# Opening of a hybrid decoder step: the first weights in two quarters, and four token transfers issued later

## The reference, cut to what matters

```python
a = rmsnorm(h, norm_mix_g)                       # h: tokens x 1024
z = a @ w_in                                     # q, k, v, gates of two branches
hm = mlstm_scan(...); hg = gla_scan(...)         # matrix memory || gated linear attention
merged = sigmoid(ga) * (hm @ w_pa) + sigmoid(gb) * (hg @ w_pb)
h = h + merged @ w_o
h = h + conv_ffn(rmsnorm(h, norm_ffn_g))         # gated FFN, width-3 causal convolution
h = h + sigmoid(rmsnorm(h, norm_ple_g) @ w_ple_gate) * (p @ w_ple_proj)
y = rmsnorm(h, final_norm_g)
```

## Time and profile before

| | us |
|---|---|
| median of three runs | 1183.09 (1182.69 to 1183.25) |
| the profiled execution | 1183.06 |
| its span | 1181.2 |
| busy PE / DVE / ACT | 1166.8 / 757.9 / 393.1 |
| first product of unit 0 | 7.90 |
| first product of unit 1 | 23.98 |

### The profile page before, as it was taken

The page is one execution under the profiler, slowest core; times in us unless marked ns, Lnnn a source line. Parts: engine busy times, 40 slices in busy tenths (PEclk is TensorE's granted clock), DMA queues, the critical chain, the costliest instruction groups (busy, mean ns, idle before and its releaser), DMA issues.

```text
span 1181.2 us, 21812 instructions
## 1 busy us (share of the span) xinstructions
PE 1166.8 (99%) x9169; PEld 1110.0 (94%) x9169; DVE 757.9 (64%) x1396; ACT 393.1 (33%) x576; POOL 2.3 (0%) x7
## 2 busy tenths in 40 slices
PE   9999999999999999999999999999999999999996
PEld 8999999999999999999999999999999999999995
DVE  6855568675777655664655667777777763333777
ACT  6243232134343322333343233333333322111544
POOL 0000000000000000000000000000000000000000
PEclk9999999999999999999999999999999999999998
DMA  6342232422312366563443542232222143223222
GB/s 220 112 145 90 90 108 90 144 72 93 113 67 109 133 228 212 177 199 120 153 155 114 172 147 72 72 108 72 75 105 72 61 163 107 72 94 98 77 99 81
DMA packets 48962, 138.56 MB, mean 117 GB/s; under 512 B 5460, under 2 KB 25108, under 8 KB 39776
## 3 DMA queue, kind: packets, MB, share of 16 engines
q1 hardware_dynamic: 16392, 89.39, 21.9%
q10 hardware_dynamic: 32472, 47.77, 12.0%
HBM read 113.15 MB, written 23.81 MB: 116 GB/s over the span
## 4 chain that ended last, share of the span: by engine, by line
PE 95%; issue 3%; DVE 1%; DMA 1%; ACT 1%; POOL 0%; ACTq 0%; POOLq 0%; DVEq 0%
PE ps L768 34%; PE ps L796 10%; PE ps L794 6%; PE ps L797 6%; PE ps L795 6%; PE ps L897 6%; PE ps L774 6%; PE ps L798 5%; PE ps L903 3%; PE ps L815 2%; PE aux L1060 1%; DMA xT<-in_xT 1%; PE aux L1124 1%; PE aux L955 1%; PE aux L1020 1%
## 5 line engine op out<-in xcount | busy, mean ns | idle before, releaser
L768 PE MATMUL ps<-apair,whi 128*128 128x288 f32 x1728 | 274.9, 298 | 0.6 <-ACT mq L2067 0.5
L768 PEld LDWEIGHTS ps<-apair,whi 128*128 128x128 f32 x1728 | 243.2, 188 | 4.9 <-issue 2.1
L1175 DVE TENSOR_TENSOR wlo<-wraw,whi 128x2048 fp32r<-128x2048 f32 (+1 forms) x82 | 176.1, 2147 | 74.8 <-ACT whi L1912 70.5
L1912 ACT ACTIVATE whi<-wraw 128x2048 fp32r<-128x2048 f32 (+1 forms) x87 | 156.4, 1797 | 106.2 <-PE ps L798 52.5
L796 PE MATMUL ps<-apair,whi 128*128 128x512 f32 x336 | 132.1, 393 | 0.0
L794 PE MATMUL ps<-apair,whi 128*128 128x320 f32 x336 | 105.0, 313 | 0.0
L797 PE MATMUL ps<-apair,wlo 128*128 128x320 f32 x336 | 104.2, 310 | 0.0
L795 PE MATMUL ps<-apair,whi 128*128 128x320 f32 x336 | 103.8, 309 | 0.0
L768 PE MATMUL ps<-apair,wlo 128*128 128x288 f32 x448 | 95.9, 296 | 0.0
L798 PE MATMUL ps<-apair,wlo 128*128 128x256 f32 x336 | 95.1, 283 | 0.0
L798 PEld LDWEIGHTS ps<-apair,wlo 128*128 128x128 f32 x336 | 63.2, 188 | 14.2
(11 more groups left out here) (405 smaller groups left out, 2091.5 us busy)
## 6 DMA issues: line engine op xcount, KB each, us to landing
wraw<-in_w_in SPq DMA_DIRECT2D x31, 1024.0 KB, 4.9
wraw<-in_w_up SPq DMA_DIRECT2D x21, 1024.0 KB, 4.8
gate_scratch<-stg ACTq DMA_DIRECT2D x32, 288.0 KB, 2.8
gt<-gate_scratch ACTq DMA_DIRECT2D x32, 288.0 KB, 2.9
wraw<-in_w_pgate SPq DMA_DIRECT2D x6, 1024.0 KB, 4.8
wraw<-in_w_down SPq DMA_DIRECT2D x8, 704.0 KB, 4.1
wraw<-in_w_down SPq DMA_DIRECT2D x8, 640.0 KB, 3.8
out_C_s<-st ACTq DMA_DIRECT2D x16, 256.0 KB, 2.8
```

Source lines behind the costliest of these rows:

```text
L768: mm = nc.tensor.matmul(ps[:, t % 2, a, 0:HALF], w, x(k)[:, a * HALF:(a + 1) * HALF], start=f, stop=e)
L1175: V.tensor_tensor(wlo[:, s, 0:n], wraw[:, s, 0:n], f32(whi[:, s, 0:n]), ALU.subtract)\
L1912: A.activation(whi[:, s, 0:n], wraw[:, s, 0:n], ACT.Copy).then_inc(split_hi, 1)
```

## The change

The first half of unit 0 arrives in two quarters. The first quarter (blocks 0 and 1, 256 KB) is SyncE's first transfer, ahead of the gains; the second (blocks 2 and 3) follows the gains. VectorE rounds the first quarter itself, before it waits for the gains; ScalarE rounds the second quarter behind block 1. The low parts of the quarters are made by VectorE behind blocks 0 and 1. ScalarE's queue issues only the first token piece ahead of the Sqrt with its table load, and the other four behind it. In `first_unit` TensorE takes the four products with `ahi` before the four with `alo`, and waits for `alo` only between them; it waits for the second quarter at block 2.

```diff
--- before.py
+++ after.py
@@ -431,8 +431,9 @@
             return [sem(f"{name}{i}") for i in range(n)]
 
         raw_in = sems("raw_in", 2)
-        raw_first = sem("raw_first")
+        raw_first = sems("raw_first", 2)
         hi_first = sem("hi_first")
+        hi_second = sem("hi_second")
         lo_first = sem("lo_first")
         ones_set = sem("ones_set")
         misc_in = sem("misc_in")
@@ -582,6 +583,10 @@
             x, k0 = both[0 if k < 4 else 1 if k < 6 else 2]
             return x[:, k - k0, :]
 
+        def quarter(q):
+
+            return slice(q * UW // 4, (q + 1) * UW // 4)
+
         def half_of(e):
             return slice(TS * e, TS * (e + 1))
 
@@ -615,7 +620,6 @@
 
         @block.sync
         def _(sp):
-            sp.dma_start(gains[:, :, :], ins["gains"]).then_inc(gains_in, 16)
             for u, (kind, i) in enumerate(units):
                 s = u % 2
                 if (kind, i) == ("ga", 0):
@@ -633,7 +637,9 @@
                     sp.wait_ge(split_hi, u - 1)
                     sp.wait_ge(split_lo, u - 1)
                 if u == 0:
-                    sp.dma_start(wraw[:, 0, 0:UW // 2], ins["w_in"][0, :, 0:UW // 2]).then_inc(raw_first, 16)
+                    sp.dma_start(wraw[:, 0, quarter(0)], ins["w_in"][0, :, quarter(0)]).then_inc(raw_first[0], 16)
+                    sp.dma_start(gains[:, :, :], ins["gains"]).then_inc(gains_in, 16)
+                    sp.dma_start(wraw[:, 0, quarter(1)], ins["w_in"][0, :, quarter(1)]).then_inc(raw_first[1], 16)
                     sp.dma_start(wraw[:, 0, UW // 2:], ins["w_in"][0, :, UW // 2:]).then_inc(raw_in[0], 16)
                     sp.dma_start(misc_raw[:, :, :], ins["w_misc"]).then_inc(misc_in, 16)
                 else:
@@ -832,20 +838,21 @@
                 for k in range(KT):
                     if k == 0:
                         pe.wait_ge(hi_first, 1)
+                    elif k == 2:
+                        pe.wait_ge(hi_second, 1)
                     elif k == KT // 2:
                         pe.wait_ge(split_hi, 1)
                         pe.wait_ge(split_lo, 1)
-                    pe.wait_ge(a_hi, k + 1)
-                    pe.wait_ge(a_lo, k + 1)
-                    for n in range(2):
-                        col = (2 * k + n) * P
-                        for x in (ahi, alo):
+                    for x, ready in ((ahi, a_hi), (alo, a_lo)):
+                        pe.wait_ge(ready, k + 1)
+                        for n in range(2):
+                            col = (2 * k + n) * P
                             for a in range(2):
                                 nc.tensor.matmul(ps[:, t + n, a, 0:HALF], whi[:, 0, col:col + P],
                                                  x[:, k, a * HALF:(a + 1) * HALF],
                                                  start=k == 0 and x is ahi, stop=False)
-                    if k == 0:
-                        pe.wait_ge(lo_first, 1)
+                    if k in (0, 2):
+                        pe.wait_ge(lo_first, k // 2 + 1)
                     for n in range(2):
                         col = (2 * k + n) * P
                         for a in range(2):
@@ -1467,14 +1474,16 @@
             for s in sched:
                 j, t = job_at[s], tile_at.get(s)
                 if s[0] == "norm_in":
+                    dve.wait_ge(raw_first[0], 16)
+                    V.tensor_copy(whi[:, 0, quarter(0)], wraw[:, 0, quarter(0)]).then_inc(hi_first, 1)
                     dve.wait_ge(gains_in, 16)
                     for k in range(KT):
                         dve.wait_ge(a_hi, k + 1)
                         V.scalar_tensor_tensor(alo[:, k, :], xT[:, k, :], gains[:, NORM_MIX, k:k + 1],
                                                f32(ahi[:, k, :]), ALU.mult, ALU.subtract).then_inc(a_lo, 1)
-                        if k == 0:
-                            dve.wait_ge(hi_first, 1)
-                            V.tensor_tensor(wlo[:, 0, 0:UW // 2], wraw[:, 0, 0:UW // 2], f32(whi[:, 0, 0:UW // 2]),
+                        if k < 2:
+                            dve.wait_ge((hi_first, hi_second)[k], 1)
+                            V.tensor_tensor(wlo[:, 0, quarter(k)], wraw[:, 0, quarter(k)], f32(whi[:, 0, quarter(k)]),
                                             ALU.subtract).then_inc(lo_first, 1)
                         elif k == 3:
                             dve.wait_ge(split_hi, 1)
@@ -1992,10 +2001,11 @@
                 act.wait_ge(aux_free[bank_of[j]], use_of[j])
                 act.sem_inc(h_out, 1)
 
-            for n, (k0, k1) in enumerate(X_PIECES):
-                act.dma_start(xT[:, k0:k1, :], ins["xT"][:, k0:k1, :]).then_inc(x_in[n], 16)
+            act.dma_start(xT[:, 0:1, :], ins["xT"][:, 0:1, :]).then_inc(x_in[0], 16)
             act.wait_ge(init_done, 1)
             A.activation(stat[:, 0, :], stat[:, 1, :], ACT.Sqrt).then_inc(act_warm, 1)
+            for n, (k0, k1) in enumerate(X_PIECES[1:]):
+                act.dma_start(xT[:, k0:k1, :], ins["xT"][:, k0:k1, :]).then_inc(x_in[n + 1], 16)
             act.wait_ge(act_warm, 1)
             act.wait_ge(gains_in, 16)
             for s in sched:
@@ -2006,9 +2016,9 @@
                         for k in range(k0, k1):
                             A.activation(ahi[:, k, :], xT[:, k, :], ACT.Copy, scale=gains[:, NORM_MIX, k:k + 1])\
                                 .then_inc(a_hi, 1)
-                            if k == 0:
-                                act.wait_ge(raw_first, 16)
-                                A.activation(whi[:, 0, 0:UW // 2], wraw[:, 0, 0:UW // 2], ACT.Copy).then_inc(hi_first, 1)
+                            if k == 1:
+                                act.wait_ge(raw_first[1], 16)
+                                A.activation(whi[:, 0, quarter(1)], wraw[:, 0, quarter(1)], ACT.Copy).then_inc(hi_second, 1)
                             elif k == 3:
                                 act.wait_ge(raw_in[0], 16)
                                 A.activation(whi[:, 0, UW // 2:], wraw[:, 0, UW // 2:], ACT.Copy).then_inc(split_hi, 1)
```

## The result

The changed kernel takes 1185.34 us (median of 14 executions, 1183.73 to 1186.45), the kernel before 1182.77 us (14 executions, 1182.21 to 1184.78) on the same chip: a ratio of 1.0019 [1.0011, 1.0027]. It is 2.6 us slower, outside the forecast range of 1181.4 to 1183.8.

The account below looks back on a forecast made before the run. The opening was taken as bound by a DMA landing, then from 11.1 us a serial ScalarE/VectorE chain to `mq`; the rest by TensorE. Second weight half rounded 0.6 us earlier: 1183.06 - 0.6 = 1182.5 us, range 1181.4 to 1183.8.

Parts of the forecast that it names:

- x1 is ready at 3.6, before turn 1 ends: Opening DMA: second token transfer, issued at 2.55 us, needs about 1 us to start, so it joins the second turn.
- turn 1: Opening DMA: first token transfer paired with the first weight quarter, 544 KB, ending at 4.3 to 4.6 us.
- order of turns: Opening DMA, queues alternating: x0 with first quarter, x1 with gains, x2 with second quarter, x3 with h1, x4 with misc.
- turn 2: Opening DMA: second token transfer paired with gains, 312 KB, 0.8 to 1.25 us, ending at 5.1 to 5.9.
- turn 3: Opening DMA: third token transfer paired with the second weight quarter, 832 KB, 2.1 to 2.5 us, ending at 7.2 to 8.4.
- the slower of my two rates: Opening DMA: 250 KB/us, against 390, as bounds for the first 1.1 MB.
- Rival C: Opening: the split pushes h1 (second weight half) a turn back, to land at 11.5; +0.4 us, 1183.5; chance 0.08.
- The binding chain: ScalarE/VectorE up to `mq`: h1's rounding starts at 10.5 instead of 11.10, everything to unit 1 moves 0.6 us earlier.
- Rival A: Opening: SyncE's queue gets ahead, h1 pairs with x2, blocks 2 and 3 done 0.1 to 1.1 us earlier; 1182.0; chance 0.17.
- TensorE's gain: First unit: misc ends at 22.35, 1.1 us earlier, only a ceiling, since TensorE then waits for `mq`.
- Rival D: Opening: TensorE's longer wait, 1.1 to 1.6 us, lets its clock fall to the lower level; 1185.5; chance 0.02.
- From 23.98 on all is the same program, and keeps the shift: After the opening: the same TensorE-bound program, so the 0.6 us shift at unit 1 remains to the end.

Follow-up runs that it names:

- a1: The changed kernel run again with no edit; 3.13 us above the kernel before, ratio 1.0024.
- a3: Changed kernel with all five token transfers issued at once, so only the quarters part (gains second) is new; 2.71 us above the kernel before, ratio 1.0019.
- b2: Kernel before with ScalarE copying the first tile to `mq` twice; 1.30 us above the kernel before, ratio 1.0012.
- c1: Kernel before with ScalarE copying `mq` ahead of its last two squares, their sums later in unit 1; 4.97 us above the kernel before, ratio 1.0038.
- b3: a3 with seven products of ones behind the misc products, in the wait for `mq`; 0.86 us above the kernel before, ratio 1.0008.
- f1: Kernel before with the second weight half issued by ScalarE's queue between the third and fourth token transfers; 0.28 us below the kernel before, ratio 0.9999.
- g3: Changed kernel with the first two token transfers issued at once, three behind the Sqrt; 2.87 us above the kernel before, ratio 1.0024.
- f2: Changed kernel with all tokens issued at once and the second weight half on ScalarE's queue; 1.12 us above the kernel before, ratio 1.0010.
- f3: f2 with five products of ones behind the misc products, in the wait for `mq`; 0.17 us above the kernel before, ratio 1.0002.

## Why the prediction was wrong

**Where the time went.** Three parts of the 2.6 to 3.1 us are known. The chain to unit 1 is 0.69 us later (both traces of the changed kernel). The two steps are 0.36 and 0.38 (0.37 and 0.36 in a1). That makes 1.4, and the kernels with `mq`'s wait filled measured 1.47 and 1.62 (medians; the traces of these two are of slower executions, with x2 at 11.3 and 10.8). The fall of the clock is 1.5 us in the executions that have it. By their mean clock these are at least 8 of 24 (median 1186.26); the ten with 0.996 or more have a median of 1184.84, 1.4 below, which fits the price of a fall. But these ten are still 2.1 to 2.3 above the kernel before, so that 0.7 us of the changed kernel's loss is in none of the three parts. The 0.6 that a1's trace loses near 475 us may be some of it; that was not tried. In a3 the account closes better: 0.34 and 0.7 are 1.0, and its five executions at 0.996 or more have a median 1.25 above.

**The step that failed first: "x1 is ready at 3.6, before turn 1 ends".** The issue was at 2.56 as worked out. The estimate of 1 us from issue to start came from gains and x0 on idle queues at the start of the program; x1's first bytes came 3.5 us after its issue. The prediction's order of turns therefore did not come about in the changed kernel; it did in a3, where x1 was issued at once. There it was 1.2 us and more too early: turn 1 ended at 5.8 for a forecast of 4.3 to 4.6, turn 2 at 7.0 for 5.1 to 5.9, turn 3 at 9.6 for 7.2 to 8.4. Nearly all of that is turn 1, whose 232 KB more took 2.0 us for 0.6 to 0.9, so even the slower of my two rates was too fast for it; turns 2 and 3 took 1.2 and 2.6 us for 0.8 to 1.25 and 2.1 to 2.5. With turn 1 late, h1 came at 11.41, as Rival C (chance 0.08) had it: chain +0.34 for +0.4.

This step alone would not have put the time outside the range: 1183.06 + 0.69 is 1183.75. What did are the fall of the clock and the two steps, below.

**The binding chain.** The forecast had blocks 2 and 3 done at 9.8 and h1's rounding at its landing, 10.5. h1 landed far earlier, at 8.0, and was no limit; x2 was, at 10.42, with x1 at 8.97 ahead of it holding up both block 1 and q1's rounding on ScalarE. The rounding of h1 came at 11.80, 1.3 later than forecast; unit 1 at 24.66 for 23.4. Rival A had the premise right, that SyncE's queue gets ahead, and the sign wrong: it gave the time won to x2, but misc as well as h1 landed ahead of x2. The chain from h1's rounding on did move as one piece, by 0.69.

**What held.** Gains at 5.2 (5.2; by luck, as they came 3.8 us ahead of x1 and not with it), the first token rounding at 5.25 (5.3), the cast 0.43 us (0.45), the quarter's subtraction 0.68 (0.61 to 0.7), q1's rounding 0.62 (0.6), block 0 at 6.60, ahead of 7.35, in part because the clock rose a microsecond earlier than in the trace of before. TensorE's gain was a ceiling only, as said, and a3 shows it: misc 0.75 earlier, all of it turned into a wait.

**Rival D, given 0.02: "TensorE's longer wait lets its clock fall".** The argument against it was one row: after a wait of 1.50 us late in the kernel the clock stayed at 1.00. That was one trial of something that does not come out alike each time. Of the eighteen traces here, eleven have a wait of 0.85 us or more in the first 35 us after the first unit has begun, and in six of them the clock fell, 0.5 to 2.3 us after the wait had ended; of the seven with no such wait none did. Waits of that length between the warm-up products and the first unit (b2 1.84 us, c1 1.72, b3 1.19, f1 1.15, g3 0.86) brought no fall behind them, so the length of a wait alone does not decide. The clock's own moment varies too: it rose anywhere from 3.9 to 7.3 us, though the warm-up starts at 1.05 in every trace. The changed kernel itself is in the first group twice, once with and once without. The price per fall, 1.5 us (a1, f2) to 3.0 (a3, of which 0.8 came back by 57 us), was judged rightly, 2.4 us for it; the chance was not: 8 of 24 executions at least.

**"From 23.98 on all is the same program, and keeps the shift".** It loses 0.7 us more, in two steps, because VectorE's program has become longer by three instructions and other work now stands at the late places. A sign was among the rows: the cast at 37.89 with 0.55 us idle ahead of it, ended by VectorE's own instruction. The term should have stood as an unknown, as on any edit that changes an engine's number of instructions.

## What to carry to other kernels

Making the work in front of a wait finish earlier is not free when the wait stays: TensorE's gain of 0.75 us in a3 became a wait of 1.58 us, and the clock fell in at least 5 of 11 executions, in the traced one for four times the gain. Before an opening is sped up, look at what ends last behind it (here ScalarE's chain to `mq`), or fill the wait with products that nobody needs; look at the mean granted clock of every execution too, since one trace can miss a fall that comes in a third of them. The spread of the times is a weaker sign: f2's is 3.2 us and f3's 0.8, but f1, which has neither wait nor low clock, has 2.5. When an edit adds or removes instructions on an engine, look for instructions that start late with nothing to wait for, 256 apart, and for what stands there afterwards. And time a transfer that is issued into busy queues by a row of such a transfer, not by the first ones of the program.

## What the runs showed of the hardware

- The granted clock fell from 1.00 to 0.50 in six of eleven traces with a wait of TensorE of 0.85 to 1.82 us in the first 35 us, and 1.39 us (the changed kernel) passed without a fall where 0.85 (f2) did not. A fall of 3.4 us cost 1.5 us of this kernel's time. With the wait ahead of unit 1 filled, none of 44 executions had a mean clock of 0.994 or less; without the fill, 8 of 24 of the changed kernel had.
- Single VectorE instructions start some 0.35 to 0.4 us late, at number 63 of its program and multiples of 256 further on (319, 1087, 1599, 1855, counted from 0 among the recorded ones), where the timing lets it show, in all eighteen traces. Three instructions more on VectorE, in its first 2.5 us, put other work at those numbers, and TensorE lost 0.35 us each at 589 and 1158 us.
- With one 512 KB transfer split in two and the gains second, and the same bytes in all, the last of the opening's transfers landed at 13.5 (a3) instead of 12.7, and the first 544 KB at 5.8. It also landed at 13.3 in f1, where nothing is split and h1 is on the other queue, so the split is not the only thing that does it.
- x1 issued at 2.56 us, with three or four transfers issued on the other queue before it, landed between 8.1 and 9.6 us in seven traces (first bytes between 4.75 and 6.05); issued at 1.19 it landed between 6.5 and 7.1 in the other eleven.
